# First expert stage: half of the down projection as three float32r products of high and low parts

## The reference

```python
def swiglu(t, wg, wu, wd):
    return (jax.nn.silu(t @ wg) * (t @ wu)) @ wd
...
    def expert_block(args):
        tok_b, w_b, e = args
        yb = swiglu(t_pad[tok_b], w_gate[e], w_up[e], w_down[e])
        return yb.astype(f32) * w_b[:, None]
```

## Time and profile before

| | |
|---|---|
| median of 3 runs | 2253.72 us (2251.86 to 2254.84) |
| the profiled execution's own time | 2252.88 us |
| its span | 2251.1 us |
| mean granted TensorE clock | 0.909 |
| TensorE busy over the span | 82% |
| VectorE busy | 50% |
| ScalarE busy | 35% |
| expert stage of layer 0 | about 455 to 1153 us of the span |
| expert stage of layer 1 | about 1700 to 2200 us of the span |

### The profile page before, as it was taken

How to read it: one execution, slowest core, us unless ns; L and a number is a source line. 1 busy time by engine, 2 the same in 40 slices (tenths; PEclk the granted TensorE clock), 3 DMA queues, 4 the chain that set the end, 5 groups by cost and what they waited for, 6 DMA issues and landing times. The chain is left out here.

```text
span 2251.1 us, 32259 instructions
## 1 busy us (share of the span) xinstructions
PE 1853.2 (82%) x9555; PEld 1210.6 (54%) x9556; DVE 1116.1 (50%) x1942; ACT 797.5 (35%) x1283; POOL 315.8 (14%) x333
## 2 busy tenths in 40 slices
PE   2899997979999999999966977638778778788884
PEld 0778853556767676766633961113445445455451
DVE  1425632477877777777836656891321111111113
ACT  1214511045656565666612547850101111111111
POOL 0220010011111111112211012220011111111110
PEclk9999988889999999999987988758879899999997
DMA  6860053258999999999956334304659999999984
GB/s 247 273 216 12 1 186 138 118 184 343 365 361 351 352 356 372 365 360 358 359 213 244 94 79 172 113 10 131 256 209 405 399 409 400 414 406 401 408 333 197
DMA packets 128296, 597.10 MB, mean 265 GB/s; under 512 B 32633, under 2 KB 51129, under 8 KB 67441
## 3 DMA queue, kind: packets, MB, share of 16 engines
q1 hardware_dynamic: 92512, 509.97, 58.7%
q0 software_dynamic: 35584, 84.32, 10.2%
q10 hardware_dynamic: 144, 2.10, 0.2%
HBM read 596.18 MB, written 56.20 MB: 290 GB/s over the span
## 5 line engine op out<-in xcount | busy, mean ns | idle before, releaser
L1484 DVE TENSOR_TENSOR m_w_lo<-mods,m_w_hi 128x1024 fp32r<-128x1024 f32 x264 | 311.6, 1222 | 27.4 <-ACT m_w_hi L1403 24.7
L1403 ACT ACTIVATE m_w_hi<-mods 128x1024 fp32r<-128x1024 f32 x264 | 263.7, 1049 | 13.9 <-PEq L995 12.0
L1355 PE MATMUL ps<-m_w_hi,m_x_hi 128*128 128x512 f32 x528 | 245.1, 464 | 5.6 <-DVE m_x_lo L1476 5.6
L1339 PE MATMUL ps<-m_wd,m_hidT 128*128 128x512 f32 x528 | 248.1, 592 | 0.9 <-DVE h L1492 0.9
L1702 PE MATMUL ps<-m_wd,m_hidT 128*64 128x512 f32 x528 | 163.5, 775 | 92.8 <-DMA m_wd<-in_moe_w_down 91.4
L1674 PE MATMUL ps<-m_wgu,m_xT 128*64 128x256 f32 x2112 | 236.7, 382 | 1.2 <-DVE m_xT L1768 1.2
L1674 PEld LDWEIGHTS ps<-m_wgu,m_xT 128*64 128x64 f32 x2112 | 175.0, 138 | 71.3 <-issue 21.2
L1355 PE MATMUL ps<-m_w_lo,m_x_hi 128*128 128x512 f32 x528 | 208.1, 394 | 0.0
L1355 PE MATMUL ps<-m_w_hi,m_x_lo 128*128 128x512 f32 x528 | 207.0, 392 | 0.0
L1702 PEld LDWEIGHTS ps<-m_wd,m_hidT 128*64 128x64 f32 x528 | 52.3, 176 | 180.2 <-issue 180.2
L1339 PEld LDWEIGHTS ps<-m_wd,m_hidT 128*128 128x128 f32 x528 | 95.5, 191 | 70.8 <-issue 63.6
(11 more groups left out here) (322 smaller groups left out, 3262.2 us busy)
## 6 DMA issues: line engine op xcount, KB each, us to landing
m_wd<-in_moe_w_down SPq DMA_DIRECT2D x132, 1024.0 KB, 11.1
mods<-in_moe_w_gate SPq DMA_DIRECT2D x66, 1024.0 KB, 7.0
mods<-in_moe_w_up SPq DMA_DIRECT2D x66, 1024.0 KB, 10.5
m_wgu<-in_moe_w_gate SPq DMA_DIRECT2D x66, 1024.0 KB, 11.2
m_wgu<-in_moe_w_up SPq DMA_DIRECT2D x66, 1024.0 KB, 13.5
c_rows<-y_rows SPq DMA_DIRECT2D x12, 2048.0 KB, 14.4
mods<-in_ada_w POOLq DMA_DIRECT2D x11, 1024.0 KB, 6.2
mods<-in_ada_w SPq DMA_DIRECT2D x11, 1024.0 KB, 4.9
```

The source lines that it names most:

```text
L1339: last = pe.matmul(g.ps[0:S, YB + n, :], hidT[:, q, j, :], wd[:, q, j, n * 512:(n + 1) * 512], start=(j == 0), stop=(j == KF - 1))
L1355: last = pe.matmul(g.ps[0:S, GU, :].rearrange("p (a f) -> p a f", a=2), x[:, q, k, :], w[:, q, :, k, :], start=(k == 0 and n == 0), stop=( ...
L1403: act.activation(w_hi[:, q, :, k, :], wgu[:, q, :, k, :], ACT.Copy).then_inc(hi_s, 1)
L1484: dve.tensor_tensor(w_lo[:, q, :, k, :], wgu[:, q, :, k, :], w_hi[:, q, :, k, :].bitcast(F32), ALU.subtract).then_inc(lo_s, 1)
```

## The change

In `expert_phase` half j = 0 of each block's down projection becomes three float32r products. ScalarE makes `hidT_hi` (straight from PSUM) and `wd_hi` (128x1024, one instruction, `down_high`), VectorE makes `hidT_lo` and `wd_lo` (`down_low`). `wd_hi` and `wd_lo` have one buffer each, freed by a semaphore `first_down`. Half j = 1 stays in float32. The result of a block is now copied by ScalarE alone, in one 128x1024 instruction (`copy_y`), and VectorE keeps only the row index. ScalarE's new instructions stand in its step after the `hidT` copy and ahead of `copy_y`; the wait for the down weights moves from TensorE to ScalarE's `down_high`. VectorE's stand at the end of its step, after `pick`.

At the head of the stage the tokens of block 0 are turned and split ahead of the last weight chunk, and `pick` and `indices` change order. Small tiles move into `mods_rest`. In `AdaGroups` the loads of the first group share a semaphore in pairs (`share=2`), and `project_phase` allocates `padded` only where it is used. SyncE's block is as it was.

```diff
-        self.w_in = [g.sem(f"{tag}_w_in{i}") for i in range(bufs)]
+        self.w_in = [g.sem(f"{tag}_w_in{i}") for i in range(bufs // share)]
...
-        pe.wait_ge(self.w_in[m % self.bufs], 16 * (m // self.bufs + 1))
+        pe.wait_ge(self.w_in[m % self.bufs // self.share], 16 * self.share * (m // self.bufs + 1))
...
-        act_g = sb("act_g", [S, FE])
-        hid = sb("hid", [S, FE])
-        hidT = sb("hidT", [P, 2, KF, S])
+        act_g, hid = g.mods_rest[0:S, 0, 0:FE], g.mods_rest[0:S, 0, FE:2 * FE]
+        hidT = g.mods_rest[:, 0, 2 * FE:2 * FE + 2 * S].rearrange("p (q c) -> p q c", q=2)
+        hidT_hi, hidT_lo = sb("hidT_hi", [P, 2, S], F32R), sb("hidT_lo", [P, 2, S], F32R)
+        wd_hi, wd_lo = sb("wd_hi", [P, D], F32R), sb("wd_lo", [P, D], F32R)
...
                 def down(i, q, j, first=False):
                     b = 2 * i + q
                     if j == 0:
-                        pe.wait_ge(hidT_s, b + 1)
-                        pe.wait_ge(wd_in[q], 16 * (i + 1))
+                        pe.wait_ge(hidT_split, b + 1)
+                        pe.wait_ge(wd_lo_s, b + 1)
                         if not first:
-                            pe.wait_ge(y_a, b)
-                            pe.wait_ge(y_v, b)
+                            pe.wait_ge(y_copied, b)
+                        for m, (h, w) in enumerate(((hidT_hi, wd_hi), (hidT_hi, wd_lo), (hidT_lo, wd_hi))):
+                            for n in range(2):
+                                last = pe.matmul(g.ps[0:S, YB + n, :], h[:, q, :], w[:, n * 512:(n + 1) * 512], start=(m == 0), stop=False)
+                        last.then_inc(first_down, 1)
+                        return
+                    pe.wait_ge(hidT_s, b + 1)
                     for n in range(2):
-                        last = pe.matmul(g.ps[0:S, YB + n, :], hidT[:, q, j, :], wd[:, q, j, n * 512:(n + 1) * 512],
-                                         start=(j == 0), stop=(j == KF - 1))
-                    if j == KF - 1:
-                        last.then_inc(y_done, 1)
+                        last = pe.matmul(g.ps[0:S, YB + n, :], hidT[:, q, :], wd[:, q, j, n * 512:(n + 1) * 512], start=False, stop=True)
+                    last.then_inc(y_done, 1)
...
                 slots(0, 0)
                 slots(0, 1)
+                turn_tokens(0, 0, first=True)
                 slots(1, 0)
-                turn_tokens(0, 0, first=True)
...
-                def y_half(i, q, wait=True):
+                def down_high(i, q):
+                    b = 2 * i + q
+                    act.wait_ge(wd_in[q], 16 * (i + 1))
+                    if not (isinstance(i, int) and i == 0 and q == 0):
+                        act.wait_ge(first_down, b)
+                    act.activation(wd_hi[:], wd[:, q, 0, :], ACT.Copy).then_inc(wd_hi_s, 1)
+
+                def copy_y(i, q, wait=True):
                     b = 2 * i + q
                     act.wait_ge(y_done, b + 1)
                     if wait:
                         act.wait_ge(scattered[q], 16 * i)
-                    act.activation(ysb[q][:, 0:512], g.ps[0:S, YB, :], ACT.Copy).then_inc(y_a, 1)
+                    act.activation(ysb[q], g.ps[0:S, YB:YB + 2, :].rearrange("p a b -> p (a b)"), ACT.Copy).then_inc(y_copied, 1)
...
-                    act.activation(hidT[:, q, :, :], g.ps[:, HB, 0:KF * S].rearrange("p (j c) -> p j c", c=S), ACT.Copy).then_inc(hidT_s, 1)
+                    act.activation(hidT[:, q, :], g.ps[:, HB, S:2 * S], ACT.Copy).then_inc(hidT_s, 1)
+                    act.activation(hidT_hi[:, q, :], g.ps[:, HB, 0:S], ACT.Copy).then_inc(hidT_high, 1)
+                    down_high(i, q)
                     if not (peeled and q == 0):
-                        y_half(i - 1 + q, 1 - q, wait=wait_y)
-
-                split_high(0, 0, range(CHUNKS), first=True)
+                        copy_y(i - 1 + q, 1 - q, wait=wait_y)
+
+                split_high(0, 0, range(LATE), first=True)
                 tokens(0, 0)
+                split_high(0, 0, range(LATE, CHUNKS), first=True)
...
-                    dve.wait_ge(y_done, b + 1)
-                    dve.tensor_copy(ysb[q][:, 512:D], g.ps[0:S, YB + 1, :]).then_inc(y_v, 1)
+
+                def down_low(i, q):
+                    b = 2 * i + q
+                    dve.wait_ge(hidT_high, b + 1)
+                    dve.tensor_tensor(hidT_lo[:, q, :], g.ps[:, HB, 0:S], hidT_hi[:, q, :].bitcast(F32), ALU.subtract).then_inc(hidT_split, 1)
+                    dve.wait_ge(wd_hi_s, b + 1)
+                    dve.tensor_tensor(wd_lo[:], wd[:, q, 0, :], wd_hi[:].bitcast(F32), ALU.subtract).then_inc(wd_lo_s, 1)
...
                     if not first:
-                        y_half(i - 1 + q, 1 - q, wait=not first_y)
+                        row_index(i - 1 + q, 1 - q, wait=not first_y)
                     pick(i + 2, q)
+                    down_low(i, q)
 
                 pick(0, 0, wait=False)
+                indices(0, 0, wait=False)
                 pick(0, 1, wait=False)
-                indices(0, 0, wait=False)
                 indices(0, 1, wait=False)
+                split_low(0, 0, range(LATE))
+                tokens(0, 0)
+                split_low(0, 0, range(LATE, CHUNKS))
                 pick(1, 0)
                 indices(1, 0)
                 pick(1, 1)
-                split_low(0, 0, range(CHUNKS))
-                tokens(0, 0)
```

More of the change, by code:

```diff
@@ L172, with __init__ @@
     TILES = 4
-    def __init__(self, g, tag, groups, bank, w, row, gains):
-        self.g, self.groups, self.bank, self.bufs = g, groups, bank, len(w)
+    def __init__(self, g, tag, groups, bank, w, row, gains, share=1):
+        self.g, self.groups, self.bank, self.bufs, self.share = g, groups, bank, len(w), share
         self.count = len(groups) * KD
@@ L208, in load @@
         src = self.g.ins["ada_w"][layer].rearrange("(p k) n -> p k n", k=KD)[:, k, part * self.W:(part + 1) * self.W]
-        q.dma_start(self.w[m % self.bufs], src).then_inc(self.w_in[m % self.bufs], 16)
+        q.dma_start(self.w[m % self.bufs], src).then_inc(self.w_in[m % self.bufs // self.share], 16)
     def project(self, pe, m):
@@ L252, in ada_phase @@
         wbuf, arow, again = sb("ada0_w", [P, KD, 2 * D]), sb("ada0_row", [P, 1, 512]), sb("ada0_gains", [P, 512])
-        ada = AdaGroups(g, "ada0", [(0, 0)], 0, [wbuf[:, m, :] for m in range(KD)], arow, again)
+        ada = AdaGroups(g, "ada0", [(0, 0)], 0, [wbuf[:, m, :] for m in range(KD)], arow, again, share=2)
         c_ready, c_silu, cs_clear = g.sem("ada_c_ready"), g.sem("ada_c_silu"), g.sem("ada_cs_clear")
@@ L746, in project_phase @@
         gated_s, added = g.sem(tag + "_gated_s"), g.sem(tag + "_added")
-        padded = [g.sem(f"{tag}_padded{i}") for i in range(2)]
+        padded = [g.sem(f"{tag}_padded{i}") for i in range(2)] if rows > kp else []
         ada = None
@@ L1219, in expert_phase @@
         silued, hid_s, hid_turned, hidT_s = (sem(n) for n in ("silued", "hid_s", "hid_turned", "hidT_s"))
-        y_done, y_a, y_v, sidx_s, zeroed, issue, meta_v = (sem(n) for n in ("y_done", "y_a", "y_v", "sidx_s", "zeroed", "issue", "meta_v"))
+        y_done, y_copied, sidx_s, zeroed, issue, meta_v = (sem(n) for n in ("y_done", "y_copied", "sidx_s", "zeroed", "issue", "meta_v"))
         hi_s, lo_s, chunk_used = (sem(n) for n in ("hi_s", "lo_s", "chunk_used"))
+        hidT_high, hidT_split, wd_hi_s, wd_lo_s, first_down = (sem(n) for n in ("hidT_high", "hidT_split", "wd_hi_s", "wd_lo_s", "first_down"))
         GU, YB, XB, HB, MB = 0, 1, 3, 5, 6
@@ L1275, in scatter @@
                     b = 2 * i + q
-                    pool.wait_ge(y_a, b + 1)
-                    pool.wait_ge(y_v, b + 1)
+                    pool.wait_ge(y_copied, b + 1)
                     pool.wait_ge(sidx_s, b + 1)
@@ L1366, in step @@
                         pe.wait_ge(hidT_s, b)
+                        pe.wait_ge(hidT_split, b)
                     after_wait(pe)
@@ L1420, in step @@
                         act.wait_ge(hid_s, b)
-                    act.activation(act_g[:], g.ps[0:S, GU, 0:FE], ACT.Silu).then_inc(silued, 1)
+                    act.activation(act_g, g.ps[0:S, GU, 0:FE], ACT.Silu).then_inc(silued, 1)
                     if split:
@@ L1443, in _ @@
                 step(final, 1, split=False)
-                y_half(final, 1)
+                copy_y(final, 1)
             @block.vector
@@ L1484, in split_low, with row_index @@
                         dve.tensor_tensor(w_lo[:, q, :, k, :], wgu[:, q, :, k, :], w_hi[:, q, :, k, :].bitcast(F32), ALU.subtract).then_inc(lo_s, 1)
-                def y_half(i, q, wait=True):
+                def row_index(i, q, wait=True):
                     b = 2 * i + q
@@ L1504, in step @@
                         dve.wait_ge(hid_turned, b)
-                    dve.scalar_tensor_tensor(hid[:], act_g[:], meta[:, bass.ds(b, 1), GAIN], g.ps[0:S, GU, FE:2 * FE],
```

(3 more changed lines are left out.)

## The result

The changed kernel takes 2334.22 us (median of 4 runs, 2317.21 to 2344.85) against 2254.28 us for the kernel before (4 runs, 2251.86 to 2256.54), 1.0348 times as long, 95% interval 1.0281 to 1.0414. The forecast was 2308 us, 1.024 times. The profiled execution is the shortest of the four: 2317.21 us, span 2315.4, that is 64.3 us more of both than before.

The account below looks back on a forecast made before the run. The prediction took the expert stage as TensorE-bound, VectorE and DMA near their end. From 2252.9 us, + 57 (down-weight wait) - 3 (stage head) + 1.8 (`AdaGroups`) gave 2308 us, 2.4% slower; eight in ten between 2270 and 2345.

Parts of the forecast that it names:

- The wait that moves: Expert stage: ScalarE, now waiting for the down weights itself, stands 4.0 us by today's landing times, holding up later work.
- D: Time from a gate load's issue to the landing of the down load behind it: 13.9 us before, taken as 12.2.
- P: Time of one block in the expert stage: 10.28 us before, forecast 11.2, 0.92 more in 62 blocks.
- The ring without D: Expert stage, two blocks: steps from landed down weights to the next gate load but one, summed to 10.2 us.
- The small parts: Stage head: `x_lo` no longer waits for four `w_lo` chunks, -3 us; first `AdaGroups`: shared semaphores delay a group, +1.8 us.
- The faster rival: Expert stage: the loads catch up, D falls to 10.0 and the time to 2239 us; chance 0.05.
- TensorE ring of 9.93 to 10.03: Expert stage: TensorE's own time per block in us, once the cheaper first down half saves 0.35 us.
- The ring of 10.07: Expert stage: the dependent steps through ScalarE and VectorE take 10.07 us a block, alone leaving a gain of 0.21.
- The clock rival: Expert stage: idle gaps lower TensorE's clock to 0.85, 37 us on top, 2345 us; chance 0.12 together with a steady backlog.
- The lighter queue: Expert stage, slower but less: D = 11.0, P = 10.6, 20 us more, 2272 us; chance 0.12.
- The signs: Profile after: ScalarE waits 1.5 to 2.5 us in some 62 blocks, gate loads 11 us apart, DMA share about 0.85.

Follow-up runs that it names:

- wait_only: The kernel before with only ScalarE's wait for a block's down weights moved to after the `hidT` copy, no new work: 2299.8 us, 1.022 times.
- half_early: The changed kernel with down weights loaded in two halves, the split half going out a block earlier: 2254.04 us, 1.0006 times the kernel before.
- changed_again: The changed kernel run once more without any edit: 2328.67 us, 1.0343 times the kernel before.
- reordered: half_early with `wd_hi` ahead of the `hid_turned` wait, a later block's first `w_hi` chunk ahead of `copy_y`, `pick(1, 0)` ahead of the weight split: 2257.81 us.
- head_only: The kernel before with only the stage head reordered: block 0's tokens ahead of the last chunk, `pick(1, 0)` kept ahead of the weight split: 2247.69 us.
- share_only: The kernel before with only the shared semaphores of the first `AdaGroups` (`share=2`): 2252.89 us, 1.0005 times.
- less_tensor_work: The kernel before with each down projection's second half cut from 512 to 32 columns: 2269.37 us with 70 blocks in layer 1, not 66.
- fewer_bytes_same_order: reordered without the second down half's load (512 KB a block), other loads at their old moments: median block 10.03 us against 10.44.
- earlier_issue: reordered with gate and up loads in two parts, slices 0 to 5 issued after the third `w_lo` chunk, semaphore shared over four loads: 2271.29 us.

## Why the prediction held, and where its terms were off

**The wait that moves: right, and shown.** That ScalarE would stand for the down weights in its own step, with `copy_y` and the next weight split queued behind, is in the first line of its waits. wait_only and half_early show from both sides that the loss hangs on this wait: it alone costs 48 us, and without it the new work costs nothing that can be measured.

**D: mis-sized by 0.5 us, and one block's P taken for all.** I took 12.2 us from a row at the stage's start (11.9) and one with a full backlog (13.9). Measured were 12.7 and 13.0 in two profiles. The ring without D came to 9.9 where I had summed 10.2: `copy_y` starts 0.97 us behind `wd_hi` and `w_hi` 0.90 behind `copy_y` (716.74, 717.71, 718.61), where I had 1.05 and 1.03. For the profiled execution the two nearly cancel, which is luck: P = 11.31 against 11.2. The median lies 26 us above the forecast. 9 of them are in this profile already: a block took 10.24 us on average before, not the 10.28 of the one I had read, so each is 1.07 us longer and not 0.92. The other 17 lie between this shortest run and the median. In changed_again a longer D makes most of the difference; for the longer runs of the first four no profile says whether it is D or the clock. The spread from run to run was not in my working at all: I drew the point from one execution's rows. An estimate from the figures of the Trainium skill ("DMA: Bandwidth & Descriptors", Anatomy of one DMA), which states them for one transfer on GpSimd's path, had 9.2 us for the three loads. With D at 12.7 and 13.0 the traces do not bear it out for SyncE's queue in use.

**The small parts: both wrong.** In the sum they stood at -3 and +1.8 us; in the profile they are -0.3 us and nothing, so that they nearly cancelled in either case. "Up to 3.6 us. I take 3" for the head came out as 0.3 us (469.67 against 469.93). `x_lo` did come earlier, at 465.03, but TensorE's slot lookup of block 2 stands ahead of its first product, and it waits for `pick(1, 0)`, which the change had put behind the weight split on VectorE. reordered and head_only moved it back and got the 3 us. The 1.8 us in `AdaGroups` were 1.5 us at the first group's sum (37.31 against 35.78), 1.3 at `rstd` (48.74 against 47.47), and gone by the expert stage (453.85 against 453.99); share_only finds nothing either.

**The faster rival: right that it would not come, wrong in its price.** It was to give 2239 us if the loads kept pace. half_early takes the wait away and gives 2254. I had counted a TensorE ring of 9.93 to 10.03 and one of ScalarE and VectorE of 10.07, and left out that with 3 MB a block the transfers hold P near 10.2 by themselves, though the earlier trace rows had the share of 0.92 in them. less_tensor_work (10.19 with much less for TensorE to do) and fewer_bytes_same_order (10.03 with 512 KB less) show it. The ring of 10.07 itself was not tested alone.

**The clock rival** played no part: 0.98 granted over the stretch with about 1.06 us of idle time a block (60.3 us in 57 blocks). **The lighter queue** (D = 11.0) did not come: D was at or under 11.0 in one block of each profile (11.0 and 10.8), and 12.7 and 13.0 on average.

**The signs** I had named are there: waits of 1.8 us in 52 of 57 blocks (forecast 1.5 to 2.5), gate loads 11.3 apart, DMA share 0.85, six products in 1.37 us. The ones that failed are the first product, 0.3 us earlier and not 3, and the end of the first `AdaGroups`, 1.5 us later and not 1.8.

## What to carry to other kernels

When a change moves a wait for a load to another engine or to an earlier step, compare the load's landing time with the new moment first, and then go round the ring: what that engine holds up is often what frees the buffer for the next load, and the load's time from issue to landing is then paid in full once a round (here, once in two blocks). Before taking work off an engine that is busy all the time, look at how much the transfers of the same block would allow; with a share of 0.92 the answer may be nothing. A piece that frees its buffer early can have its own, earlier load, and that alone paid back the whole loss here.

## What was not expected of the hardware

- The share of busy DMA engines is not a full measure of what is left. In reordered the share is 0.94, and P fell by 0.4 us (median block) when bytes were taken away; in earlier_issue a share of 0.95 carried 346 GB/s, while in the earlier trace rows 0.99 carries 401, 11% more for each busy share. In this stage 1 MB weight loads and the indirect gathers and scatters share the engines.
- The same kernel's block length differed by 0.14 us between two executions (11.31 and 11.45) with an equal granted clock in the stage, along with its landing times (D 12.7 and 13.0). The changed kernel's 8 runs lie within 28 us, the 13 runs of the kernel before that were taken beside the second four within 8 us (2247.66 to 2255.35). That a ring through a load's landing is what spreads more is likely and not shown.
